# Rotation taken up three slabs later, six modulation buffers, turned weights copied before the exponentials

## The reference

```python
proj = a @ w_in                       # 528 tokens (16 meta + 512) x 3584 columns
aq, ak, av, rq, rf, ri, rg = split(proj)
q, k = apply_rope(aq), apply_rope(ak) # 4 heads, two halves of 64 each
# per head and block of 128 queries, over all keys up to the block's end:
p = softmax(where(mask, q k^T, neg))  # for both halves
w = p[0] - lam * p[1]
out = w @ v
```

## Time and profile before

| | |
|---|---|
| median of 3 runs | 2997.11 us (2992.84 to 2998.12) |
| the profiled execution | 2993.14 us, its span 2991.3 us |
| PE busy over the span | 2646.0 us (88%) |
| DVE busy | 1864.1 us (62%) |
| ACT busy | 1274.5 us (43%) |
| mean granted TensorE clock | 0.957 of full speed |

### The profile page before, as it was taken

One profiled execution on the slowest core, in us unless ns is written; L12 is line 12 of the kernel. 1 busy time (PEld: TensorE's weight loads), 2 busy tenths in 40 slices (PEclk: granted clock), 3 DMA queues, 4 the chain that ended last, 5 costly groups with the idle time before them and its releaser, 6 DMA issues. The chain is left out here.

```text
span 2991.3 us, 32478 instructions
## 1 busy us (share of the span) xinstructions
PE 2646.0 (88%) x11426; PEld 1806.9 (60%) x11426; DVE 1864.1 (62%) x3850; ACT 1274.5 (43%) x2823; POOL 660.4 (22%) x638
## 2 busy tenths in 40 slices
PE   6997897988889777799999999799798788999998
PEld 6876675434444222355555555598685456788887
DVE  5786638777777677777777776554645755343323
ACT  2144225444444444465566554443243255232222
POOL 2210003334444343444444434000000100000000
PEclk9998989999999999999999999999997798999999
DMA  6753037999999999999999999555220101222332
GB/s 209 275 198 106 14 106 278 419 418 412 420 419 408 421 412 417 416 412 411 420 415 410 413 412 417 188 187 165 86 85 17 37 23 62 87 72 97 99 104 73
DMA packets 131731, 750.81 MB, mean 251 GB/s; under 512 B 17408, under 2 KB 17936, under 8 KB 65248
## 3 DMA queue, kind: packets, MB, share of 16 engines
q0 software_dynamic: 81824, 575.43, 47.3%
q1 hardware_dynamic: 49744, 173.30, 16.8%
HBM read 746.57 MB, written 2.10 MB: 250 GB/s over the span
## 5 line engine op out<-in xcount | busy, mean ns | idle before, releaser
L1782 PE MATMUL peer_y<-rows,diag 128*128 128x512 f32 x2048 | 995.6, 613 | 174.3 <-ACT diag L1762 162.8
L1736 DVE CUSTOM_DVE_ANT_0 rows<-rows,hidden 128x1024 f32<-128x1024 f32 x512 | 627.7, 1226 | 370.0 <-DMA rows<-in_peer_table,experts 365.3
L1723 POOL DMA_INDIRECT rows<-in_peer_table,experts x512 | 579.2, 1131 | 1009.1 <-PE peer_y L1782 802.6
L1782 PEld LDWEIGHTS peer_y<-rows,diag 128*128 128x128 f32 x2048 | 362.6, 192 | 588.8 <-ACT diag L1762 293.6
L1759 ACT ACTIVATE hid<-hid 128x1 f32<-128x1 f32 x512 | 102.6, 200 | 537.1 <-DVE hid L1736 532.5
L2385 DVE TENSOR_TENSOR piece_w_low<-piece_raw,piece_w_high 128x1024 fp32r<-128x1024 f32 x132 | 161.1, 1223 | 102.4 <-ACT piece_w_high L2380 102.2
L1762 ACT ACTIVATE diag<-ident,hid 128x128 f32<-128x128 f32 x512 | 205.6, 401 | 16.7
L2380 ACT ACTIVATE piece_w_high<-piece_raw 128x1024 fp32r<-128x1024 f32 x132 | 138.6, 1052 | 107.8 <-PE out_bank L152 77.6
L1760 ACT ACTIVATE hid<-hid,gates 128x1 f32<-128x1 f32 x512 | 150.8, 295 | 16.6
L417 ACT ACTIVATE proj_w_high<-proj_raw 128x1024 fp32r<-128x1024 f32 (+2 forms) x57 | 57.6, 1012 | 217.4 <-PE proj_pair L152 118.1
L150 PE MATMUL peer_y<-peer_feat_high,early_w_high 128*128 128x256 f32 x352 | 144.2, 410 | 2.0 <-issue 2.0
(11 more groups left out here) (545 smaller groups left out, 5581.2 us busy)
## 6 DMA issues: line engine op xcount, KB each, us to landing
ada<-in_w_ada POOLq DMA_DIRECT2D x96, 384.0 KB, 4.4
piece_raw<-in_ffn_w_gate SPq DMA_DIRECT2D x44, 512.0 KB, 3.6
piece_raw<-in_ffn_w_up SPq DMA_DIRECT2D x44, 512.0 KB, 4.5
piece_raw<-in_ffn_w_down SPq DMA_DIRECT2D x44, 512.0 KB, 4.3
query_raw<-in_peer_w_query SPq DMA_DIRECT2D x32, 512.0 KB, 6.9
early_raw<-in_ffn_w_gate SPq DMA_DIRECT2D x22, 512.0 KB
early_raw<-in_ffn_w_up SPq DMA_DIRECT2D x22, 512.0 KB
early_raw<-in_ffn_w_down SPq DMA_DIRECT2D x22, 512.0 KB
```

Source lines behind the costliest of these rows:

```text
L1723: pool.indirect_dma_start(self.rows[:, b, :], None, self.table, bass.IndirectOffsetOnAxis(ap=self.experts[:, unit % self.SETS, n % TOPK:n ...
L1736: dve.tensor_tensor_reduce(out=self.rows[:, b, 0:D], in0=self.rows[:, b, 0:D], in1=self.hidden[:, tile, :], scale=1.0, scalar=0.0, op0=ALU ...
L1782: last = pe.matmul(self.y[self.bank(tile)][:, c * BANK:(c + 1) * BANK], self.diag[:, b, :], self.rows[:, b, D + c * BANK:D + (c + 1) * BAN ...
```

## The change

Five edits, all in this block:

- `TURN_AT` puts TensorE's product for block b after slab 2b+2 instead of 2b+3, and `TURN_LAG` 3 instead of 1 puts VectorE's `rotate(b)` into the step of slab 2b+5 instead of 2b+4.
- The modulation ring has six buffers instead of four in the plain steps (still two in the units). GpSimd issues six pieces before it issues the three rotation tables.
- The matrix of the swap lies elsewhere in memory, to make room.
- In the attention units ScalarE's `move_turned(u-1)` stands before the exponentials of u.
- In each unit one modulation instruction stands behind `maxima(u)`; odd units keep their other one before it. The number in each unit is as before.

```diff
--- before.py
+++ after.py
@@ -581,14 +581,13 @@
     PLAIN = ALL - LATE
     E_LATE = len(moves) - N
     RING_BANKS = 6
-    TURN_AT = {2 * b + 3: b for b in range(2 * AH)}
-    TURN_LAG = 1
+    TURN_AT = {2 * b + 2: b for b in range(2 * AH)}
+    TURN_LAG = 3
     ADA_PLAIN = 72
-    DEEP, DEEP_LATE = 4, 2
+    DEEP, DEEP_LATE = 6, 2
     with ExitStack() as ctx:
         gap = Scratch(nc, nc.sbuf_base, LIMIT)
         in_late = Scratch(nc, late_at, late_at + 4 * 2 * RH * NT)
-        rope_turn = in_late.sbuf("turn", [P, P])
         rope_cos = in_late.sbuf("cos", [P, NT])
         rope_sin = in_late.sbuf("sin", [P, NT])
         ada = [(gap if i < DEEP_LATE else in_late).sbuf(f"ada{i}", [P, ACH]) for i in range(DEEP)]
@@ -598,6 +597,7 @@
         prob = in_gate.sbuf("prob", [P, 2, 2, NT])
         w_meta = in_gate.sbuf("w_meta", [NM, 2, P])
         stat = in_gate.sbuf("stat", [P, 2, 2, 6])
+        rope_turn = in_gate.sbuf("turn", [P, P])
         w_turned = Scratch(nc, t.meta_at, t.meta_at + 4 * D).sbuf("w_turned", [P, 2, TT, P])
         weight = [in_gate.sbuf("weight0", [P, NT]), gap.sbuf("weight1", [P, NT])]
         mask = gap.sbuf("mask", [P, P])
@@ -810,6 +810,8 @@
                     weights.split_high(act, n + weights.RING)
                 if u >= 2:
                     move_out(u - 2)
+                if u >= 1:
+                    move_turned(u - 1)
                 for half in range(2):
                     act.wait_ge(max_ready, 2 * u + (2 if long(u) else half + 1))
                     if u >= 2:
@@ -818,8 +820,6 @@
                         last = act.activation(prob[:, u % 2, half, at:at + m], src, ACT.Exp, bias=stat[:, u % 2, half, 1:2],
                                               scale=scale, accum_out=stat[:, u % 2, half, 2 + c:3 + c])
                     last.then_inc(exp_done, 1)
-                if u >= 1:
-                    move_turned(u - 1)
             move_out(N - 2)
             move_turned(N - 1)
             move_out(N - 1)
@@ -892,10 +892,12 @@
                 n = PLAIN + u // 2
                 if u >= 1:
                     weigh(u - 1)
-                if u % 2 == 0 and n + 1 < ALL:
+                if u % 2:
+                    modulation(ADA_PLAIN + u + (u + 1) // 2)
+                elif n + 1 < ALL:
                     weights.split_low(dve, n + 1)
-                modulation(ADA_PLAIN + (N_ADA - ADA_PLAIN) * (u + 1) // N)
                 maxima(u)
+                modulation(ADA_PLAIN + u + 1 + (u + 1) // 2)
             weigh(N - 1)
 
         weights.close()
```

## The result

The changed kernel takes 2977.09 us (median of 5, 2975.78 to 2981.62) against 2997.11 (median of 5, 2992.84 to 3001.45): the ratio is 0.9942, 95% interval 0.9931 to 0.9953. Forecast were 2979 us and faster. In a second series on another occasion the same kernel had 2979.2 us and 0.9945 (0.9932 to 0.9959).

What follows compares the result with a forecast made beforehand. PE was taken to bound the projections and the order of DVE's queue attention; 6.3 (rotation), 8.8 (modulation) and 1.3 us (tail) sum to 16.4, taken from a mean of 2995.3 to give 2979 us, range 2971 to 2989.

Steps and rivals of the forecast that it cites:

- The term of 6.3 us: Projections: moving product and rotation removes all of PE's idle time waiting for L423, 6.3 us, bounds 0 and 7.
- The six buffers at 0: Projections: two more modulation pieces in flight cut DVE's waits off PE's path, so they gain 0 us.
- a round of 23.7 us: Attention: DVE's time between two long units' L874 falls from 26.4 by 2.7 to 23.7 us.
- 0.2 us a round: Attention: allowance for DVE reaching the maxima before the scores are there, 0.2 us per round, 0.6 in all.
- The 0.5 us a round for the refill of a buffer: Attention: wait for a freed buffer of the two-buffer ring to be filled again, 0.5 us, 1.5 in three rounds.
- my term of 8.8 us: Attention: gain from modulation behind the maxima, 11.5 us less three deductions, leaving 8.8; bounds 4 and 12.
- the 10.1 forecast: Attention: what is won without the projections' gain, 8.8 us from modulation behind the maxima and 1.3 at the tail.
- The turned weights: Attention: copies first save 1.3 us at the tail, bounds 0 and 2, and let PE follow the shorter rounds.
- Rival A: Attention: PE becomes the bound, slow clock stretches cost 5 us, 2984 us; sign: rounds over 25 us, PE 0.9 busy; 14%.
- B: Projections win nothing because DVE's wait for modulation pieces sets the pace; 10.1 us won, 2985 us; 9%.
- C: Block's gain is given back in later blocks through DMA and clock; within 0.2%, about 2994 us; 11%.
- D: Attention: the two-buffer ring becomes the chain of the units and the kernel is slower, about 3003 us; 4%.

Runs made afterwards that it cites:

- rot_lag_only: Kernel before with only TURN_LAG 2 instead of 1 (rotation one step later on VectorE, product not moved): ratio 0.9972, projections 128.51 us.
- after_again: The changed kernel profiled once more with no edit: three rounds of 23.66 us, no slow stretch in them.
- six_only: Kernel before with only six modulation buffers instead of four and the swap matrix moved: ratio 0.9999, projections 136.65 us.
- defer_turn: Changed kernel where TensorE, after a long unit, does the second half of the late slab before that unit's transposes: ratio 0.9930.
- rot_only: Kernel before with only the change's TURN_AT and TURN_LAG (four buffers, units as before): 2987.39 us, ratio 0.9977.
- turned_only: Kernel before with only move_turned ahead of the exponentials: ratio 1.0003.
- turned_again: Kernel before with only move_turned ahead of the exponentials, run a second time for its profile: rounds of 26.27, 26.08 and 26.23 us.
- before: The profiled execution of the unchanged kernel: span 2991.3 us; the kernel's median of 5 is 2997.11 us.
- mods_only: Kernel before with only one modulation instruction per unit moved behind the maxima: ratio 0.9987.
- units_only: Kernel before with only both edits of the attention units (copies first, modulation behind the maxima): 2982.71 us, ratio 0.9954.
- last_short: Changed kernel with the last head's query blocks in the order 2, 3, 1, 0, so the last unit is shortest: ratio 0.9937.

## Why the prediction was right, point by point

The direction and the size are right: 16.4 us were forecast for the profiled execution's span, and the spans differ by 16.0; the ratio of 0.9942 is 17.4 us of 2997.11, and the medians differ by 20.0. The terms were less even than the sum.

The projections. The step was right: DVE late behind the rotation product, with over 3 us of cover once moved. The term of 6.3 us measured 7.15 between the marks, just over its bound of 7, and is the difference of two misses. The stall was worth 8.3 us, as `rot_lag_only` shows: the 6.3 us of idle time and another 0.3 us, not 0.1, in each of the seven stalled slabs. That I put the cost of the product's move on TensorE at nothing was a miss of 1.1 us with six buffers and 1.7 with four. A further 1.46 us came ahead of the first mark, from a clock that rose earlier in that execution; that was luck in the profile, and `after_again` did not have it (44.33).

The six buffers at 0: 0.1 us alone, 0.55 us with the rotation. Right as a size (one execution each); the reason too, since `six_only` shows the saved wait reappear as a wait for the product.

The modulation instructions: forecast was a round of 23.7 us, measured were 23.65 or 23.66 in eight rounds of four executions without a slow stretch in them (but the tail's). The number is right, two of its parts are not, and they cancelled. I took 26.40 us as the round of before, while 0.75 of the second round was its slow stretch; and I allowed 0.2 us a round for DVE coming before the scores, while it waits 1.0 us for them:

```profile
DVE stat L874 <- ACT prob L820: 2.2, 2, 1.1
PE rot_bank L735 <- DVE weight L880: 1.7, 1, 1.7
DVE rot_bank L860 <- PE rot_bank L727: 0.6, 1, 0.6
DVE proj_pair L860 <- PE proj_pair L727: 0.4, 1, 0.4
```

These are waits of the second round after (217.47 to 241.12 us). The window holds the L874 waits of both its ends, so one of them, 1.1 us, belongs to the round. The 0.5 us a round for the refill of a buffer was in my term of 8.8 us but not in the 23.7, and it did not come: the units' waits of the changed kernel have no row of DVE waiting for pieces. By the Trainium skill (SBUF — State Buffer, the "DVE blocks DMA" trap) a DMA issued from GpSimd can be held by certain DVE instructions. No such delay shows in this trace: the pieces issued from 182 to 262 us landed after 3.5 us in the median and 4.6 at most, against 3.7 and 5.2 before.

That the DVE queue is the chain of a round held before and only in part after. In the third round DVE has one L423 less (busy 19.51 instead of 20.55 us in `after_again`), and the round is no shorter, as it waits 2.0 us for scores instead of 1.0: the way through TensorE, which first stands 1.7 us for the long unit's weights, sets it as well, and `defer_turn`, which changes only TensorE's order, takes 0.8 us off each round. Ahead of the first L874 the units went from 22.60 us at full clock (`rot_only`) to 20.25, with TensorE busy for 20.19: there TensorE is the bound, which I had only as a rival.

The 10.6 us that the units won in `after_again` are 2.5 ahead of the first L874, 6.7 in the three rounds and 1.4 at the tail. Some 1.4 to 1.9 us of it are slow stretches that the profile of before had and this one did not, so the edits give about 9 us against the 10.1 forecast.

The turned weights: 1.3 us at the tail. The tail of the changed kernel from L874 is 6.85 us, before 8.23: 1.4. By themselves they bring the rounds nothing that `turned_only` or `turned_again` shows; with DVE earlier they let TensorE follow, 0.4 to 0.5 us of a round.

Rival A happened in part. In the first profile a slow stretch fell into two of three rounds and cost 1.5 and 1.3 us, so the units won 7.9 us of 10.1; the first of them is the sign I had given for A, a round over 25 us with TensorE busy for 0.9 of it (25.19 and 0.93). Without one, in `after_again`, they won 10.6 (108.85 to 98.26). I had put it at 14% as a whole outcome, while each round has its own chance of it; and I had written that the slow stretches cost nothing before, while they cost 0.75 us of the second round, 0.3 to 0.75 of the first and 0.4 ahead of it. By the Trainium skill (TensorE: Matmul & The Clock Gate, HAM oscillation) idle gaps bring the clock down and steady work releases it. The runs agree in direction, and show it as a matter of chance: a slow stretch came with or within 2 us behind TensorE's waits of 2.6 to 3.3 us in six of six (`turned_only`, `turned_again`), those of 2.0 to 2.1 us, for copies, in six of 14 (`before`, `rot_only`, `rot_lag_only`, `six_only`, `mods_only`), those of 1.3 to 1.9 us in three of twelve (the changed kernel twice, `units_only`, `last_short`), and in the three rounds of `defer_turn`, whose longest wait is 0.8 us, in none before the tail's. Two more slow stretches, at 191.2 us in `before` and at 217.8 us in `rot_only`, came about 2 us behind waits of only 1.1 to 1.2 us.

B, C and D did not happen: DMA's share rose to 0.85 in the projections and TensorE waited for nothing of it, and the rest of the program took 0.5 us longer.

## What to carry to other kernels

Look for what stands in order ahead of a late instruction, not for how busy its engine is: here VectorE was three quarters busy and yet stopped TensorE seven times, because one instruction in its queue waited for a product that was issued a moment before. Work that nobody waits for belongs between an engine's request to another and the use of the answer. A wait that is moved off the chain may gather in one place on TensorE and be paid as a slower clock; try such an edit together with the one that shortens the chain, and judge an execution by its rounds at full clock.

## What the runs showed of the hardware that was not expected

TensorE's clock decides 0.75 to 2.2 us of a round by whether a slow stretch falls into it, taking like rounds together: 0.75 in the second of before and in the third of `six_only` (25.58 against 24.83), 1.5 and 1.3 in the changed kernel, and 2.2 in `rot_lag_only` (27.89 against 25.65), where it lasted some 6.8 us. It differs between executions of the same program: the changed kernel had two such stretches in one profile and none in the next. The moment at which the clock first rose moved the first mark between 42.40 and 44.93 us over all runs, 2.5 us that belong to no edit: in the changed kernel's first profile it rose at 37.8 us and the mark came at 42.40, in its second at 40.6 and 44.33.
